# Cached attention of a decoder step: from float32r high and low parts to plain float32 in four column groups

## The reference

```python
for g, (w, d) in enumerate(A_GROUPS):
    nk = w // d + 1
    dist = jnp.arange(nk, dtype=jnp.int32) * d
    idx = buf_lens[g] + t0 + jnp.arange(qb, dtype=jnp.int32)[:, None] - dist[None, :]
    kg = jnp.take(ext_k[g], idx, axis=1).astype(jnp.float32)
    vg = jnp.take(ext_v[g], idx, axis=1).astype(jnp.float32)
    s = (jnp.einsum('bqhd,bqkhd->bhqk', qblk[:, :, g], kg) * scale
         - slopes[g][None, :, None, None] * dist.astype(jnp.float32)[None, None, None, :])
```

## Time and profile before

| | |
|---|---|
| median of 3 runs | 919.87 us (919.61 to 920.91) |
| the profiled execution | 920.17 us |
| its span | 918.3 us |
| mean granted TensorE clock | 0.993 of full speed |
| TensorE (PE) busy | 896.5 us, 98% |
| VectorE (DVE) busy | 554.4 us, 60% |
| ScalarE (ACT) busy | 321.7 us, 35% |
| GpSimd (POOL) busy | 214.1 us, 23% |

### The profile page before, as it was taken

How to read it: one execution, slowest core, us unless ns; L and a number is a source line. 1 busy time by engine, 2 the same in 40 slices (tenths; PEclk the granted TensorE clock), 3 DMA queues, 4 the chain that set the end, 5 groups by cost and what they waited for, 6 DMA issues and landing times.

```text
span 918.3 us, 19353 instructions
## 1 busy us (share of the span) xinstructions
PE 896.5 (98%) x6844; PEld 836.5 (91%) x6844; DVE 554.4 (60%) x1013; ACT 321.7 (35%) x512; POOL 214.1 (23%) x179
## 2 busy tenths in 40 slices
PE   7999999999999999999999999999989999999996
PEld 7999999999999999997887887887859999999996
DVE  4348634773467346747787797796776333333377
ACT  4133403350235123444454453553454222222110
POOL 0028202820182019233044034034010000000003
PEclk9999999999999999999999999999989999999998
DMA  7999899688969896764794793794787878877712
GB/s 227 201 277 330 304 183 270 234 312 157 284 219 333 153 288 214 253 208 145 265 330 143 252 345 125 262 357 136 245 305 244 284 264 276 273 262 275 238 53 104
DMA packets 163820, 221.04 MB, mean 241 GB/s; under 512 B 9089, under 2 KB 136833, under 8 KB 162049
## 3 DMA queue, kind: packets, MB, share of 16 engines
q1 hardware_dynamic: 158944, 207.09, 73.1%
q0 software_dynamic: 4176, 11.02, 3.6%
q10 hardware_dynamic: 656, 2.36, 0.7%
HBM read 207.71 MB, written 100.01 MB: 335 GB/s over the span
## 4 chain that ended last, share of the span: by engine, by line
PE 89%; DVE 5%; DMA 2%; issue 1%; ACT 1%; POOL 0%; SPq 0%; POOLq 0%; DVEq 0%; ACTq 0%
PE bank L761 21%; PE bank L762 20%; PE bank L763 20%; PE bank L1060 6%; PE bank L756 6%; PE bank L791 4%; PE bank L886 2%; PE bank L861 2%; PE bank L1108 2%; PE bank L1022 1%; DVE part_l L1741 1%; PE bank L1122 1%; PE bank L1132 1%; PE bank L1099 1%; DMA cslot<-in_cache_kv_w_dram 1%
## 5 line engine op out<-in xcount | busy, mean ns | idle before, releaser
L761 PE MATMUL bank<-xh,wh 128*128 128x288 f32 x640 | 192.0, 300 | 0.6 <-DVE vn L1579 0.6
L763 PE MATMUL bank<-xh,wl 128*128 128x288 f32 x640 | 188.6, 295 | 0.0
L762 PE MATMUL bank<-xl,wh 128*128 128x288 f32 x640 | 188.5, 294 | 0.0
L761 PE MATMUL bank<-wh,xh 128*128 128x256 f32 x640 | 184.6, 289 | 1.1 <-DVE qk L1707 0.6
L762 PE MATMUL bank<-wl,xh 128*128 128x256 f32 x640 | 180.9, 283 | 0.0
L763 PE MATMUL bank<-wh,xl 128*128 128x256 f32 x640 | 180.8, 282 | 0.0
L1512 DVE TENSOR_TENSOR wl<-raw,wh 128x1024 fp32r<-128x1024 f32 (+1 forms) x104 | 130.0, 1287 | 8.5 <-ACT wh L1267 7.6
L1267 ACT ACTIVATE wh<-raw 128x1024 fp32r<-128x1024 f32 (+1 forms) x104 | 101.8, 1017 | 70.4 <-PE bank L791 42.2
L761 PEld LDWEIGHTS bank<-wh,xh 128*128 128x128 f32 x640 | 122.9, 192 | 3.1 <-DVE qk L1707 0.8
L762 PEld LDWEIGHTS bank<-wl,xh 128*128 128x128 f32 x640 | 123.0, 192 | 0.6
L763 PEld LDWEIGHTS bank<-wh,xl 128*128 128x128 f32 x640 | 123.0, 192 | 0.0
(11 more groups left out here) (219 smaller groups left out, 1718.6 us busy)
## 6 DMA issues: line engine op xcount, KB each, us to landing
raw<-in_w_in_dram SPq DMA_DIRECT2D x128, 256.0 KB
cslot<-in_cache_kv_w_dram SPq DMA_DIRECT2D x32, 1024.0 KB, 6.4
out_dram<-in_cache_kv_w_dram SPq DMA_DIRECT2D x16, 2040.0 KB, 10.0
out_dram<-in_cache_kv_w_dram SPq DMA_DIRECT2D x32, 1020.0 KB, 8.5
far<-in_cache_kv_w_dram SPq DMA_DIRECT2D x32, 512.0 KB, 10.0
out_dram<-in_cache_kv_w_dram SPq DMA_DIRECT2D x20, 504.0 KB, 10.5
raw<-in_w_in_dram SPq DMA_DIRECT2D x16, 512.0 KB
out_dram<-in_cache_kv_w_dram SPq DMA_DIRECT2D x24, 252.0 KB, 3.2
```

The lines of the kernel that those rows point to most:

```text
L761: pe.matmul(out, lhs[0](k), rhs[0](k), start=(k == 0), stop=False)
L762: pe.matmul(out, lhs[0](k), rhs[1](k), start=False, stop=False)
L763: last = pe.matmul(out, lhs[1](k), rhs[0](k), start=False, stop=(k == n - 1))
```

## The change

The cached attention works in plain float32. Each attention head gets 32 result rows, a column group of the array, of which 8 are used: the four heads' matmuls of a tile write rows 0 to 31, 32 to 63, 64 to 95 and 96 to 127 of one bank, 128 columns each. The splits go, and with them `part_h`, `part_l` and `pn`; five buffers `keyt` hold the turned keys. Row work is done on 128 partitions and 408 columns in place of 32 and 480. The own keys take 12 short matmuls, the turn of the probabilities three transposes and one matmul. `sample_state_pair` takes the place of two `sample_state_group` and multiplies two halves of 32 rows into two banks in turn. On TensorE the units that stood between the value tiles now stand before or behind them. SyncE's waits are on the new semaphores `v_used` (a slot's value tiles were multiplied), `v_done` and `key_copied`, and its loads come in another order. The unused rows of `vown` and `fars` are cleared by POOL, `qm` and `pm` by VectorE. Some padding tiles move addresses.

The diff, cut. In the parts shown, nearly all lines with a minus are left out too; they are those of the listing above.

```diff
-        part_h = [sb(f"part_h{b}", [P, H * P], F32R, scope_b) for b in range(3)]
-        part_l = [sb(f"part_l{b}", [P, H * P], F32R, scope_b) for b in range(3)]
+        keyt = [sb(f"keyt{j}", [P, H * P], F32, scope_b) for j in range(KTILES)]
         qk = sb("qk", [P, TT, 2 * RK], F32, scope_b)
...
+        qm = sb("qm", [P, Q_VARIANTS * P], F32, scope_b)
+        kown = sb("kown", [P, G * H * DEC_T], F32, scope_b)
+        srow = sb("srow", [P, COLS], F32, scope_b)
+        smx = sb("smx", [P, 4], F32, scope_b)
+        pm = sb("pm", [P, VTILES * P], F32, scope_b)
+        vown = sb("vown", [P, H * DH], F32, scope_b)
...
-                src = fscr.rearrange("h q x m -> (h q) (x m)")
-                sp.dma_start(fars[64:64 + ROWS, :], src[:, bass.ds(r * (2 * P), 2 * P)]).then_inc(far_back, 16)
+                src = fscr.rearrange("h q x m -> h q (x m)")
+                for h in range(H):
+                    sp.dma_start(fars[h * QUAD:h * QUAD + DEC_T, :], src[h, :, bass.ds(r * (2 * P), 2 * P)])\
+                        .then_inc(far_back, 16)
...
+            def keys(r, x):
+                sp.wait_ge(v_used[0], r * 2 + (x + 1))
+                load_tiles(r * 2 + x, 0, 0)
+            def near_values(r, x):
+                sp.wait_ge(tg_done, r * B_TG + (TG_B + KTILES * x + KTILES))
+                load_tiles(r * 2 + x, 1, 0)
+            def far_values(r, x):
+                for slot in (1, 2):
+                    sp.wait_ge(v_used[slot], r * 2 + (x + 1))
+                    load_tiles(r * 2 + x, 1, slot)
+            def own_values(r, x):
+                sp.wait_ge(v_done, r * 2 + (x + 1))
                 for g in range(G):
                     w = GROUPS[g][0]
...
+                    src = kv_s[g][bass.ds(r * 2 + x, 1), w - DEC_T:w, 1, :, :].rearrange("b t h d -> (b t) (h d)")
+                    sp.dma_start(vown[g * DEC_T:(g + 1) * DEC_T, :], src).then_inc(vown_in, 16)
             def gate_chunk(c, f):
...
             sp.wait_ge(far_free, H + 1)
+            sp.wait_ge(kd_done, 1)
+            keys(0, 0)
             far_scores(0)
...
+            far_values(0, 0)
             states(0)
             def stage_b(r, last):
...
+                near_values(r, 0)
+                settle(sp)
+                own_values(r, 0)
+                rows(2, A_COPY_B - 1, r * 510, 255)
+                keys(r, 1)
                 sp.wait_ge(states_out, r + 2)
                 if last:
                     gate_chunk(C0_C, 0)
                 else:
                     settle(sp)
                     retention_chunk(r * B_CH + (C0_B + 2), r + 1, 0)
...
+                far_values(r, 1)
+                near_values(r, 1)
                 if not last:
                     retention_chunk(r * B_CH + (C0_B + 3), r + 1, 1)
...
+                own_values(r, 1)
                 rows(2, A_COPY_B - 1, r * 510 + 255, 255)
                 rows(1, A_COPY_B - 1, r * 126, 126)
                 rows(0, A_COPY_B - 1, r * 30, 30)
...
                     sp.wait_ge(rt_free[1], r * 9 + 6)
                     settle(sp)
                     head_constants(r + 1)
...
+                    keys(r, 2)
                     sp.wait_ge(rows_max, r * 2 + 2)
                     settle(sp)
                     far_scores(r + 1)
...
+                    far_values(r, 2)
                     states(r + 1)
...
             own.after(pool.memset(half[:, :], -0.5))
+            own.after(pool.memset(vown[:, :], 0.0))
+            own.after(pool.memset(fars[:, :], 0.0))
             pool.memset(qdm[:, :], 0.0).then_inc(kd_done, 1)
...
                     def score_tile(j):
...
+                        pe.wait_ge(key_copied, r * (2 * KTILES) + (KTILES * x + j + 1))
+                        g, variant = (0, 0) if j == 0 else (1, G + j - 1)
                         for h in range(H):
...
+                            o = variant * P + h * QUAD
+                            last = pe.matmul(bank[4][quad(h), g * P:(g + 1) * P], qm[:, o:o + QUAD],
+                                             keyt[j][:, h * P:(h + 1) * P], start=(j < 2), stop=(j in (0, KTILES - 1)))
+                        if j == KTILES - 1:
+                            last.then_inc(key_used, 1)
+                    for j in range(2, KTILES):
+                        transpose_tile(r, x, j)
                     pe.wait_ge(qm_done, r * 2 + (x + 1))
                     settle(pe)
...
                     for j in range(KTILES):
...
                         score_tile(j)
+                    for g in range(G):
+                        for h in range(H):
+                            o, n = g * P + h * QUAD, (g * H + h) * DEC_T
+                            at = OWN_AT + g * DEC_T
+                            last = pe.matmul(bank[4][quad(h), at:at + DEC_T], qm[:, o:o + QUAD], kown[:, n:n + DEC_T],
+                                             start=True, stop=True)
+                    last.then_inc(cs_done, 1)
+                def cached_probs(x):
                     pe.wait_ge(co_read, r * 2 + (x + 1))
                     settle(pe)
...
                     pe.wait_ge(rows_norm, r * 2 + (x + 1))
                     settle(pe)
...
+                def cached_output(x):
                     pe.wait_ge(cp_read, r * 2 + (x + 1))
                     settle(pe)
                     for i in range(VTILES):
...
+                        if i == TILES:
+                            pe.wait_ge(vown_in, r * (2 * 16 * G) + 16 * G * (x + 1))
+                        for n, (lo, hi) in enumerate(SLOTS):
+                            if i == lo:
+                                pe.wait_ge(slot_in[n], r * 128 + (64 * x + 64) if n == 0 else r * 64 + (32 * x + 32))
+                                settle(pe)
+                            if lo <= i < hi:
+                                s, k = n, i - lo
+                        v = vown[:, :] if i == TILES else cslot[s][:, k, :]
+                        for h in range(H):
+                            o = i * P + h * QUAD
+                            last = pe.matmul(bank[4][quad(h), 0:DH], pm[:, o:o + QUAD], v[:, h * DH:(h + 1) * DH],
+                                             start=(i == 0), stop=(i == TILES))
+                        if i == TILES:
+                            last.then_inc(v_done, 1)
+                        elif i + 1 == SLOTS[s][1]:
+                            last.then_inc(v_used[s], 1)
                 def cached_turn(x):
...
+                    pe.wait_ge(co_copied, r * 2 + (x + 1))
                     settle(pe)
...
+                    turn(bank[5][:, 0:P], srow[:, 0:P]).then_inc(ct_done, 1)
...
+                def sample_state_pair(n):
+                    out = [group(5 + n), group(6 + n)]
                     settle(pe)
                     for x in range(2):
...
+                        for g in range(2):
+                            o = (STATE_AT[n + g] + x) * RK
+                            rows = slice(g * NS // 2, (g + 1) * NS // 2)
+                            i = pe.matmul(out[g][:, x * RV:(x + 1) * RV], km[rows, o:o + RK], vr[rows, QBLK, :],
+                                          start=True, stop=True)
+                            if x == 1:
+                                i.then_inc(rt_done, 1)
...
+                sample_output()
+                sample_state_pair(0)
+                value_unit(4)
+                sample_state_pair(2)
+                cached_output(0)
+                att_group()
+                cached_turn(0)
                 transpose_tile(r, 1, 0)
                 transpose_tile(r, 1, 1)
                 state_group(0)
...
                 state_group(1)
                 cached_scores(1)
                 output_group(0)
...
                 next_unit(0)
                 cached_probs(1)
                 next_unit(1)
...
+                next_unit(2)
+                cached_output(1)
+                next_unit(3)
+                next_unit(4)
+                pe.wait_ge(normed, r + 1)
+                for e in range(2):
+                    b = group(14 + e)
+                    blocks(lambda t, c: turn(b[:, c], ro[:, t, e * P:(e + 1) * P]))
+                cached_turn(1)
                 if not last_head:
                     transpose_tile(r + 1, 0, 0)
                     transpose_tile(r + 1, 0, 1)
...
                     turn(b[:, 0:NS], ro[0:NS, QBLK, e * P:(e + 1) * P]).then_inc(rt_done, 1)
                 if last_head:
                     first_gate(1, KT_N // 2)
...
                 for j in range(first, end):
...
+                    if j == 0:
+                        act.wait_ge(key_used, r * 2 + (x + 1))
+                        settle(act)
                     act.wait_ge(tg_done, r * B_TG + (TG_B + KTILES * x + j + 1))
...
+                    act.activation(keyt[j][:, :], bank[KEY_BANK[j]][:, :], ACT.Copy).then_inc(key_copied, 1)
...
+                key_tiles(r, 0, 2, KTILES)
                 rows(0)
...
                 queries(r, 1)
```

(52 more changed lines are left out.)

278 lines of the change are left out of this document (65 added, 213 removed).

## The result

The changed kernel takes **894.76 us** (median of four runs, 891.77 to 896.5) against 920.01 (919.61 to 920.91): ratio 0.9721, interval 0.9694 to 0.9748. The forecast was 891.8, in a range of 878 to 912. The profiled execution took 891.77, 3 us less than the median.

What follows compares the result with a forecast made beforehand. TensorE, busy 98% of the span, was taken as the bound. Three ordinary heads (-19.2 us) and the last (-8.9) gave -28.1 from 920.2; less 0.3 to the median, 891.8 us, range 878 to 912.

Steps and rivals of the forecast that it cites:

- Packing: Cached attention matmuls: four column groups run side by side, so a slot of four 128-column records costs 0.109 us.
- A: Rival, cached attention matmuls: loads or issue hold the groups, a slot costs 0.22 us; 911 us, chance 0.14.
- B: Rival, cached attention matmuls: groups run one after another, a slot costs 0.43 us; 968 us, slower; chance 0.05.
- E: Rival, whole change: it gains nothing, only if packing fails at 0.24 us a slot; 918 to 921 us, chance 0.02.
- Outputs: Cached outputs: 28 slots and 0.5 us of entry and waits a sample, against 7.3 before; 7.5 us saved a head.
- scores: Cached scores, paced by ScalarE's copies: 3.5 us against 5.0 a sample; 3.0 us saved a head.
- Probabilities: Turning the probabilities: 0.65 us against 0.4, twice; with the output's turn back, net 0.1 us lost a head.
- State pairs: Sample state matmuls with row halves together: 2.1 us for 8 slots, about 1.0 a pair; 1.8 us saved a head.
- The stall: TensorE waits 4.2 us for sample 1's keys in slot 0, then a low clock; 5.5 us lost a head together.
- The last head: Fourth retention head: -2.6 us up to sample 1's probabilities, then 15 instead of 21.3, -6.3; sum -8.9 us.
- D: Rival, loads in the heads: DMA becomes the bound and both samples stall, +3 to 4 us a head; 906, chance 0.11.
- C: Rival, the wait for sample 1's keys: it is covered or small, 18 us more saved; 874 us, chance 0.08.

Runs made afterwards that it cites:

- same_columns: The changed kernel with the output matmuls of all four heads writing the same 32 rows of the bank, result not the attention's: 931.7 us.
- the first attempt to better it: The changed kernel with sample 0's cached outputs moved on TensorE to before the samples' retention output: 891.5 us, ratio 0.9699.
- one_group: The changed kernel with cached output matmuls reordered, within each slot of tiles all of head 0, then head 1 and so on: 902.2 us.

## Why the prediction was right, and which terms were not

- **Packing** (a slot of 0.109): right. Measured 0.114 over a whole block; with one column group 12.34 us, or 0.44 a slot. Rivals A and B are out, and with them E. B's 968 was over: paying for the long block alone costs 931.7. B's break-even of 0.24 us a slot does not follow from its own terms either: 11.9 us over 76 slots is 0.157 above 0.109, or 0.27.
- **Loads** (the bound of rival A): not so. All of these matmuls take 128 rows, and even in a single column group (same_columns) they start 0.109 us apart, though each has a load of 0.110 us of its own: in the block of 12.34 us the 112 loads are busy for 12.14 us and the 112 matmuls for 12.34, so the loads run beside matmuls.
- **Outputs**: 3.2 us a sample against 3.55; **scores**: 2.8 us (466.64 to 469.49, and 503.30 to 506.10) against 3.5, because the copies follow closer than I put them. Together some 2.1 us a head better than forecast. **Probabilities**: 0.75 us a turn (448.03 to 448.78) against 0.65, and 0.34 before (418.23 to 418.57) against 0.4; with the turn back, 0.2 a head worse. **State pairs**: (488.37 - 484.31 less the 3.0 of a unit) 1.06 each, as forecast.
- **The stall**: the place, the releaser and the low clock behind it came as forecast, the sizes too small: 5.6 us against 4.2, 1.9 against 1.3. The 5.5 in the forecast's sum is the 4.2 and this 1.3, which was my estimate and which no run shows: filling the idle time was worth 1.9. "As state stores and the next weight chunk share the engines" got 0.5 us on a base of 3.7, but the prediction's own median case is 7.2 - 3.1 = 4.1, which leaves next to nothing for the sharing. The loads took 7.65, 6.65, 7.87 and 8.77 us from the second issue to landing in the chain of waits, where the earlier trace rows has a median of 6.4. Together 7.5 instead of 5.5 a head, within the bounds of 2.5 to 10.
- **What the forecast missed in the heads**: the steps costed at nothing. The sample's output and its first state pair now stand side by side, so VectorE's copy between them shows, 0.6 us; and GpSimd's rotation had less TensorE work to hide behind, 0.64. The 0.3 for the next head's keys was not spent. The stalls of the first three heads average 5.35 us, 1.2 over the forecast, and their low clock 0.6 over. The terms sum to -0.7 - 1.4 + 0.2 + 1.8 + 0.6 + 0.6 - 0.3 = 0.8 us less gain a head; 1.1 was measured (5.3 against 6.4), and 0.3 stays unexplained.
- **The last head**: from the turn of the probabilities (642.62) to the next stage's matmul (656.87) 14.2 us, against the 15 forecast; the wait for the normalised rows was 2.19 instead of 3.6. The -2.6 for the head's first part is not what its terms give: 3.75 + 3.0 + 1.8 - 5.5 is a gain of 3.0.
- **Placement**: no term at all. The unused tiles stood in the diff and I passed over them. The failing step is that the rest of the kernel was taken as untouched; the runs show 6.4 us there, against 25.3 for the whole change. In one profile of each, the attention stage takes 378.2 us without the tiles instead of 373.5, which is more than the 3.5 us that the stage gave. Without them the changed kernel would have come out at 901, inside the range but 9 from the forecast.
- **D, the DMA engines as bound**: not so at 57.5 us a head and 81%. **C**: the stall was there.

What the forecast could have said and didn't: what is late next once the stall is covered. The store of the states and the load of the weights into the same buffer, 14.7 us, cost nothing in the changed kernel and all but 3 us of the gain in the first attempt to better it.

## What to carry to other kernels

Here each head needs at most 32 result rows, and four of them in four column groups cost what one does, in plain float32: 0.114 us for a slot of four records, and 0.110 for one record where all write the same group (12.34/112). Alternate the groups: a block took 3.2 us with four in turn, 4.0 with two, 7.2 with the heads one after another and 12.3 in one group. A wait that a reordering uncovers is priced only together with the next chain behind it: list every chain that ends at the same engine, its length and its start, then order the work so that the longest is started first. Count unused tiles and other shifts of buffers as an edit of their own, and time them alone.

## What the runs showed of the hardware that was not expected

- Matmuls of different column groups overlap even where they do not alternate: with a head's ten or eight records of a slot one after another and then the next head's (one_group), a block ran in 7.24 us, not the 12.34 of a single group (same_columns), and near its start ten records start in 0.68 us, where a single series 0.109 us apart gives six.
- Filling an idle of 5.6 us on TensorE with transposes nobody reads kept the granted clock behind it at 1.00, where it had been 0.77 in the first head, and was worth 1.9 us a head.
- The same float32r matmul starts every 118 or 120 ns, and the same VectorE subtraction takes 1436 to 1515 ns, by where their buffers lie.
